# A fused three-layer block with a mixture of experts: ring places of the expert weights by order of release, and a row table made by products

## The reference

```python
pg_top, g_idx = lax.top_k(softmax(hr @ w_rg + b_rg), 1)          # one of 4 groups
pe_top, e_idx = lax.top_k(softmax(sel), 2)                        # two of its 8 experts
order = argsort(expert of each of the 1024 assignments, stable)   # rows by expert
xb = h[tokens of one expert]                                      # gathered rows
y = (silu(xb @ w_gate[e]) * (xb @ w_up[e])) @ w_down[e] * weight  # 32 experts, FF 512
out = zeros.at[token].add(y)
```

## Time and profile before

| | us |
|---|---|
| median of 3 runs | 3084.15 |
| lowest and highest | 3083.63, 3089.73 |
| the profiled execution | 3083.59 |
| its span in the profile | 3081.7 |
| TensorE busy | 2933.5 |
| VectorE busy | 1353.7 |
| ScalarE busy | 1014.0 |
| GpSimd busy | 833.0 |

### The profile page before, as it was taken

One profiled execution on the slowest core, in us unless ns is written; L12 is line 12 of the kernel. 1 busy time (PEld: TensorE's weight loads), 2 busy tenths in 40 slices (PEclk: granted clock), 3 DMA queues, 4 the chain that ended last, 5 costly groups with the idle time before them and its releaser, 6 DMA issues.

```text
span 3081.7 us, 37986 instructions
## 1 busy us (share of the span) xinstructions
PE 2933.5 (95%) x15772; PEld 2119.1 (69%) x15772; DVE 1353.7 (44%) x2292; ACT 1014.0 (33%) x1613; POOL 833.0 (27%) x431
## 2 busy tenths in 40 slices
PE   8999999999996999999999998999999999999996
PEld 6687778886675776877788777787788773333332
DVE  4443230113788754232301224143522338887884
ACT  4454442333772323334423324313332320000000
POOL 3122234442231000222344422202244421211110
PEclk9999999999998899999999999999999999999998
DMA  3341222322120002312223232111133359999995
GB/s 128 97 149 57 67 82 96 96 96 80 51 73 15 2 2 91 122 61 63 96 96 96 96 96 82 55 42 55 56 101 103 129 209 416 406 400 402 412 408 220
DMA packets 207402, 416.43 MB, mean 135 GB/s; under 512 B 16358, under 2 KB 186374, under 8 KB 194304
## 3 DMA queue, kind: packets, MB, share of 16 engines
q1 hardware_dynamic: 190992, 389.05, 34.5%
q0 software_dynamic: 16096, 24.94, 2.3%
q10 hardware_dynamic: 144, 0.01, 0.0%
HBM read 501.70 MB, written 16.79 MB: 168 GB/s over the span
## 4 chain that ended last, share of the span: by engine, by line
PE 80%; DVE 7%; DMA 7%; ACT 3%; issue 2%; POOL 1%; SPq 0%; ACTq 0%; POOLq 0%; DVEq 0%
PE product_banks L650 14%; PE product_banks L651 14%; PE product_banks L652 14%; PE product_banks L2361 7%; PE product_banks L2391 4%; DMA A<-in_w_down 4%; PE product_banks L745 2%; PE product_banks L618 2%; DMA X<-in_w_down 1%; PE product_banks L1693 1%; PE score_banks L1285 1%; PE stat_bank L877 1%; PE product_banks L1695 1%; PE product_banks L1694 1%; PE product_banks L1306 1%
## 5 line engine op out<-in xcount | busy, mean ns | idle before, releaser
L547 POOL TENSOR_TENSOR Wr_parts<-Wr,Wr_parts 128x1024 fp32r<-128x1024 f32 (+3 forms) x223 | 524.7, 2354 | 1054.3 <-ACT Wr_parts L524 1054.2
L651 PE MATMUL product_banks<-A_parts,Wr_parts 128*128 128x512 f32 x1480 | 580.3, 392 | 0.0
L524 ACT ACTIVATE Wr_parts<-Wr 128x1024 fp32r<-128x1024 f32 (+3 forms) x223 | 228.6, 1027 | 620.6 <-PE product_banks L652 569.2
L2443 DVE STREAM_TRANSPOSE Wr<-Wr 32x128 f32<-32x128 f32 (+1 forms) x752 | 388.1, 516 | 16.5 <-DMA Wr<-token_rows,from_row 5.3
L2361 PE MATMUL product_banks<-A,Wr 128*64 128x512 f32 x1328 | 338.3, 599 | 10.0 <-DMA A<-in_w_up 8.8
L651 PEld LDWEIGHTS product_banks<-A_parts,Wr_parts 128*128 128x128 f32 x1480 | 280.9, 190 | 58.0 <-issue 1.0
L650 PE MATMUL product_banks<-H_parts,Wr_parts 128*128 128x512 f32 x744 | 297.1, 399 | 3.5 <-POOL Wr_parts L547 3.5
L650 PE MATMUL product_banks<-A_parts,Wr_parts 128*128 128x512 f32 x736 | 291.9, 397 | 5.7 <-POOL Wr_parts L547 2.8
L652 PE MATMUL product_banks<-H_parts,Wr_parts 128*128 128x512 f32 x744 | 291.5, 392 | 0.0
L652 PE MATMUL product_banks<-A_parts,Wr_parts 128*128 128x512 f32 x736 | 288.6, 392 | 0.0
L547 POOL TENSOR_TENSOR shared_con_parts<-Wr,shared_con_parts 128x1024 fp32r<-128x1024 f32 (+3 forms) x83 | 191.3, 2305 | 341.9 <-ACT shared_con_parts L524 341.9
(11 more groups left out here) (540 smaller groups left out, 4768.6 us busy)
## 6 DMA issues: line engine op xcount, KB each, us to landing
A<-in_w_gate SPq DMA_DIRECT2D x29, 2048.0 KB, 13.7
A<-in_w_up SPq DMA_DIRECT2D x28, 2048.0 KB, 18.1
A<-in_w_down SPq DMA_DIRECT2D x28, 2048.0 KB, 14.5
Wr<-in_m_w_up SPq DMA_DIRECT2D x32, 1024.0 KB, 5.1
Wr<-in_m_w_down SPq DMA_DIRECT2D x32, 1024.0 KB, 4.8
Wr<-in_w_in SPq DMA_DIRECT2D x32, 1024.0 KB, 5.6
Wr<-in_c_w_kv SPq DMA_DIRECT2D x12, 1024.0 KB, 5.1
Wr<-in_b_w_rkv SPq DMA_DIRECT2D x12, 1024.0 KB, 4.8
```

The costliest lines, as they stand in the source:

```text
L524: nc.scalar.activation(weight_parts(s)[0], loaded_part(s), ACT.Copy).then_inc(*mark("weights_high", s))
L547: nc.gpsimd.tensor_tensor(lo, loaded_part(s), hi, ALU.subtract).then_inc(*mark("weights_split", s))
L651: pe.matmul(bank[:, :], hi[:, k, :], x_lo, start=False, stop=False)
L2443: ins = nc.vector.transpose(dst[32 * c:32 * c + 32, :].rearrange("p (k t) -> p k t", k=n)[:, :, rows], src[rows, 32 * n * c:32 * n * (c + ...
```

## The change

Four things are changed.

1. The row table is made on the chip. VectorE makes a matrix of ones and zeros for the place within a column (`AT_PLACE`) and one for the column, times the token's number (`IN_COLUMN`), and TensorE multiplies them (`row_ids_pe`, 8 products of 24 columns). The eight scatters, the table in main memory, its clearing and its reading back are gone.
2. `first_rows_pe` makes the rows of pair 0 in token order, 2 x 4 products of 512 columns; ScalarE copies them to `FIRST_ROWS`, TensorE turns them in 8 transposes, and ScalarE copies them to `XT` as before. `row_ids_pe` stands between the two halves.
3. The ring's places go by pairs to whole stages (`PLACES`, `places_of_stages`): when stage q is done, its pair of places goes to stage q+2 if that is an overflow stage, and otherwise to the next main stage that has none yet.
4. GpSimd waits for `extras_known` after its first two gathers, and VectorE makes `from_row` and `to_row` before the assignments' weights.

```diff
--- before.py
+++ after.py
...
+        IN_COLUMN = tmf[:, 0:8 * NCOL].rearrange("p (j c) -> p j c", j=8)
+        AT_PLACE = flat[:, 4096:5120].rearrange("p (j s) -> p j s", j=8)
+        FIRST_ROWS = shared[:, 1024:2048]
...
             link(dve, nc.vector.tensor_reduce(COLUMN, STEPS, AX_X, ALU.add))
-            link(dve, nc.vector.tensor_scalar(COLUMN, COLUMN, 1.0 - P * NCOL, None, ALU.mult))
-            link(dve, nc.vector.scalar_tensor_tensor(out=COLUMN, in0=DS, scalar=float(NCOL),
-                                                     in1=COLUMN, op0=ALU.mult, op1=ALU.add))
-            nc.vector.tensor_copy(rows_of[:, :], COLUMN).then_inc(*mark("rows_known", 0))
+            link(dve, nc.vector.scalar_tensor_tensor(out=PLACE, in0=COLUMN, scalar=float(-P),
+                                                     in1=DS, op0=ALU.mult, op1=ALU.add))
+            link(dve, nc.vector.tensor_scalar(COLUMN, COLUMN, float(CAP), None, ALU.mult))
+            link(dve, nc.vector.tensor_tensor(
+                IN_COLUMN, cc("first")[:, None, 0:NCOL].broadcast_to([P, 8, NCOL]),
+                COLUMN[:, :, None].broadcast_to([P, 8, NCOL]), ALU.is_equal))
+            link(dve, nc.vector.tensor_tensor(
+                IN_COLUMN, IN_COLUMN, cc("token")[:, :, None].broadcast_to([P, 8, NCOL]), ALU.mult))
+            for j in range(8):
+                ins = nc.vector.tensor_scalar(AT_PLACE[:, j, :], cc("place"), PLACE[:, j:j + 1], None,
+                                              ALU.is_equal)
+            ins.then_inc(*mark("rows_known", 0))
...
+            dve.wait_ge(*at("row_ids_formed", 0))
+            link(dve, nc.vector.tensor_scalar(SROW, S2[:, 1, 288:288 + NCOL], NO_ROW, None, ALU.add))
+            link(dve, nc.vector.tensor_scalar(GROW, SROW, float(T), float(-T), ALU.is_ge, ALU.mult))
+            link(dve, nc.vector.tensor_tensor(GROW, GROW, SROW, ALU.add))
+            nc.vector.tensor_copy(to_row[:, :], SROW)
+            nc.vector.tensor_copy(from_row[:, :], GROW).then_inc(*mark("row_ids_ready", 0))
...
-            dve.wait_ge(*at("row_ids_loaded", 0))
...
             pe.wait_ge(*at("first_places_ready", 0))
+            pe.wait_ge(*at("rows_ready", ("h2", TT - 1, 1)))
+            for n in range(2):
+                for m in range(TT):
+                    mm = pe.matmul(BK[:, 2 + n, :], FIRST[:, m, :], HR[:, m, n * T:(n + 1) * T],
+                                   start=(m == 0), stop=(m == TT - 1))
+                mm.then_inc(*mark("first_rows_formed", n))
+                if n == 0:
+                    row_ids_pe(pe)
             pe.wait_ge(*at("rows_ready", ("xr", TT - 1, 1)))
+            for n in range(2):
+                pe.wait_ge(*at("first_rows_kept", n))
             for k in range(8):
-                for m in range(TT):
-                    mm = pe.matmul((B6, B7)[k // 4][:, (k % 4) * P:(k % 4 + 1) * P],
-                                   HR[:, m, k:D:DT], FIRST[:, m, :], start=(m == 0),
-                                   stop=(m == TT - 1))
-            mm.then_inc(*mark("first_rows_formed", 0))
-
-        def ids_pool(pool):
-
-            pool.wait_ge(*at("rows_known", 0))
-            pool.wait_ge(*at("ids_cleared", 0))
+                mm = pe.transpose((B6, B7)[k // 4][:, (k % 4) * P:(k % 4 + 1) * P],
+                                  FIRST_ROWS[:, k:D:DT], ident)
+            mm.then_inc(*mark("first_rows_turned", 0))
+
+        def row_ids_pe(pe):
+
+            pe.wait_ge(*at("rows_known", 0))
             for j in range(8):
-                pool.indirect_dma_start(
-                    out=id_dram, out_offset=bass.IndirectOffsetOnAxis(
-                        ap=rows_of[:, j:j + 1].bitcast(U32), axis=0),
-                    in_=cc("token", j, 1), in_offset=None).then_inc(
-                        *mark("id_scattered", j, 16))
+                mm = pe.matmul(S2[:, 1, 288:288 + NCOL], AT_PLACE[:, j, :], IN_COLUMN[:, j, :],
+                               start=(j == 0), stop=(j == 7))
+            mm.then_inc(*mark("row_ids_formed", 0))
...
-        LOAD_AT = {key: g for g, key in enumerate(LOADS)}
+
+        PLACES = ((2, 3), (4, 5), (6, 0), (1, 7))
+
+        def places_of_stages():
+
+            taken, before = {}, {}
+            is_extra = [PAIRS[b][0] == "extra" for _, b in STAGES]
+            mains = [q for q in range(len(STAGES)) if not is_extra[q]]
+            for n in range(len(PLACES)):
+                taken[mains.pop(0)] = n
+            for q in range(len(STAGES)):
+                then = q + 2 if q + 2 < len(STAGES) and is_extra[q + 2] else \
+                    mains.pop(0) if mains else None
+                if then is not None:
+                    assert then > q
+                    taken[then], before[then] = taken[q], q
+            return ({STAGES[q]: PLACES[n] for q, n in taken.items()},
+                    {STAGES[q]: STAGES[n] for q, n in before.items()})
+
+        PLACE_OF, USED_BEFORE = places_of_stages()
+
+        def place_of(key):
+            return PLACE_OF[key[0:2]][key[2]]
...
+        PLACE_FREE = {2: ("products_done", ("proj2", 7)), 3: ("products_done", ("proj2", 7)),
+                      4: ("low_part_ready", ("merged", 7)), 5: ("low_part_ready", ("merged", 7)),
+                      6: ("products_done", ("proj2", 7)), 0: ("products_done", ("wout2", 7)),
+                      1: ("products_done", ("wout2", 7)), 7: ("turned", ("xr", TT - 1, 1))}
 
         def slot_free(eng, key):
-            g = LOAD_AT[key]
-            if g >= RINGW:
-                kind, b, _ = LOADS[g - RINGW]
-                eng.wait_ge(*at("unit_used", (kind, b)))
+            if key[0:2] in USED_BEFORE:
+                eng.wait_ge(*at("unit_used", USED_BEFORE[key[0:2]]))
             elif "C" in phases:
-                eng.wait_ge(*at(*SLOT_FREE[g]))
+                eng.wait_ge(*at(*PLACE_FREE[place_of(key)]))
...
-            sp.wait_ge(*at("id_scattered", 7))
-            sp.dma_start(row_ids[:, :], id_dram.rearrange("(p c) a -> p (c a)", p=P)).then_inc(
-                *mark("row_ids_loaded", 0, 16))
...
             def extras_in(*stages):
                 for key in LOADS:
-                    g = LOAD_AT[key]
-                    place = LOADS[g - RINGW][0:2] if g >= RINGW else None
-                    if PAIRS[key[1]][0] == "extra" and place in stages:
+                    if PAIRS[key[1]][0] == "extra" and USED_BEFORE[key[0:2]] in stages:
                         load_extra(pool, key)
 
-            pool.wait_ge(*at("extras_known", 0))
-            extras_in(None)
             pool.wait_ge(*at("row_ids_ready", 0))
             for m in range(TT):
                 pool.wait_ge(*at(f"h2_stored{m}", 0))
             rows_in_pool(pool, 1)
             rows_in_pool(pool, 2)
+            pool.wait_ge(*at("extras_known", 0))
             for b in range(len(PAIRS)):
...
-            act.wait_ge(*at("first_rows_formed", 0))
+            for n in range(2):
+                act.wait_ge(*at("first_rows_formed", n))
+                nc.scalar.activation(FIRST_ROWS[:, n * T:(n + 1) * T], BK[:, 2 + n, :],
+                                     ACT.Copy).then_inc(*mark("first_rows_kept", n))
+            act.wait_ge(*at("first_rows_turned", 0))
...
-            act.dma_start(id_dram.rearrange("(p c) a -> p (c a)", p=P), LB[:, 0, 0:NCOL]).then_inc(
-                *mark("ids_cleared", 0, 16))
...
-                nc.vector.memset(LB[:, :, :], 0.0).then_inc(*mark("zeros_set", 0))
```

More of the change, by code:

```diff
@@ L2246, in program @@
         LOADS = [(kind, b, h) for kind, b in STAGES for h in range(halves(b))]
-        LOAD_AT = {key: g for g, key in enumerate(LOADS)}
+        PLACES = ((2, 3), (4, 5), (6, 0), (1, 7))
[16 more added lines that the diff above has]
+            return PLACE_OF[key[0:2]][key[2]]
         def unit_slot(key):
-            place = (2, 3, 4, 5, 6, 0, 1, 7)[LOAD_AT[key] % RINGW]
+            place = place_of(key)
             return X[:, :, :] if place == 7 else A[:, 8 * place:8 * place + 8, :]
@@ L2281, in load_main @@
             sp.dma_start(unit_rows(key), src).then_inc(
-                *mark(f"unit_loaded{LOAD_AT[key] % RINGW}", key, 16))
+                *mark(f"unit_loaded{place_of(key)}", key, 16))
         def load_extra(pool, key):
@@ L2292, in load_extra @@
                 bounds_check=NE * P - 1, oob_is_err=False).then_inc(
-                *mark(f"extra_loaded{LOAD_AT[key] % RINGW}", key, 16))
+                *mark(f"extra_loaded{place_of(key)}", key, 16))
         def rows_in_pool(pool, b):
@@ L2534, in mlp_act @@
                         rectified(j)
-                    if tag == "m0" and "D" in phases and h == 0 and j == 1:
-                        clear_ids(act)
                     if h and j >= 8 and memory_ahead(tag):
@@ L3752, in _ @@
         def _(act):
-            if "D" in phases and "A" not in phases:
-                clear_ids(act)
             act.wait_ge(*at("constants_set", 0))
```

20 lines of the change are left out of this document (1 added, 19 removed).

## The result

The changed kernel takes 3184.7 us in the median of five runs (3178.3 to 3204.5), against 3084.15 for the kernel before (3082.2 to 3089.7): a ratio of 1.032 [1.030, 1.034], 3.2% slower. The forecast was 3157 in a range from 3085 to 3190.

What follows compares the result with a forecast made beforehand. TensorE and the DMA engines were both taken as near their limit, 61.8 against 61.4 us per nine stages. The sum was 3083.6 - 3.6 - 25.8 + 75.6 + 27.7 = 3157.5, so 3157 us, range 3085 to 3190.

Steps and rivals of the forecast that it cites:

- Step 1: Before the first gate: cheaper first rows and row table start it at about 2528.8 instead of 2532.39, 3.6 us gained.
- Step 2: Expert loop: main loads leave earlier, so 23.7 us of weight waits and 2.1 of clock go, 25.8 us gained.
- Step 3: Expert loop: overflow loads leave only one stage before use, so gate and down stages wait, 103 us lost.
- the eighth pair: Last overflow pair of the expert loop: no main load behind it any more, so it costs nothing.
- The waits: TensorE's waits for overflow loads: down 8.0 us, gate 2.5, up 0; first pair's gate 11.5 and down 12.
- The 14.7: Overflow pair in a loaded queue: its second load is there 14.7 us after the first issue.
- The clock: Stages after long waits run at a lower clock: 2.1 us charged per down wait and twice for the first pair.
- No waits: Rival for the overflow loads: they land within 6.5 us of issue, nothing is lost, 3054 us; chance 0.12.
- Drained queue: Rival: stalls keep the main queue short, each gate and down waits 1.8 us, 3103 us; chance 0.19.
- Worse: Rival: gate and down both find a loaded queue each time, 3180 to 3206 us; chance 0.05.
- The queue rule: DMA engines alternate one for one between GpSimd's and main loads' packets; eight turns take one main load, 4.9 us.

Runs made afterwards that it cites:

- the last experiment: Changed kernel without the 42 loads of unused overflow units, the first overflow pair's three stages taking places four stages ahead: 3065.2 us, ratio 0.994.
- the run with one: Changed kernel, loads of overflow units 1 to 14 covering 16 rows instead of 128, one packet per DMA engine instead of eight: 3112.5 us, ratio 1.009.
- the runs with shorter turns: Changed kernel, each main load issued as two DMAs of 8 KB a row (3155.5 us) or four of 4 KB (3111.0 us) instead of one of 16 KB.

## Why the prediction came out as it did

The sign, the mechanism and the place were right; the loss was 101 us where I had said 73. By its own steps:

- **Step 1, start, 3.6 gained: 4.4.** The products came near their prices: 3.7 us for four of 512 (said 3.4), 1.97 for eight of 24 (2.1). Nothing waited for VectorE ahead of the table's products, where I had allowed 0.4, and the handovers cost next to nothing of the 0.7 put in for them. What the step left out is the first gate stage: I kept its 8.6 us of the kernel before, and it took 6.9, so the start gave 6.1 in all.
- **Step 2, main loads, 25.8 gained.** In the changed kernel all 23.7 us of these waits are gone, as said. But there the stalls themselves gave the transfers time. Without stalls (the last experiment) the loop is 525.8 - 510.2 = 15.6 us shorter. Of these, 1.7 are the first stage's, and 4.9 stand in the kernel before without its empty loads as well (520.9), so some 9 are left for the order. The step was oversized: the first blocks stay bound by transfers.
- **Step 3, overflow loads, 103 lost: 134.** The stages that wait (down, gate, not up), the eighth pair with nothing, and the first gate's wait (12.4, said 11.5) came as written. With the start shifted by 16.8, the first overflow gate came at 2575 (said 2576), in part by luck: TensorE was ready 2.3 us before its time and the load left 2.5 before its own, and the two cancel. Two sizes in the step failed. *The waits:* down 9.5 us in the mean of pairs two to seven (8.9 to 10.4), said 8.0; gate 3.6, said 2.5; the first down 14.2, said 12. Together 105.4 for 86.5. In the last two rows below the first load leaves 0.8 us after its stage's end instead of 0.4, and the second is there 16.4 us after that instead of 14.7 (2806.39 less 2789.96): 0.8 + 16.4 - 6.9 = 10.3, and the wait was 10.36. The 14.7 came from a gate pair. The down pairs two to seven of the kernel before took 14.3 to 16.1 us from the first issue to the second landing, 15.4 in the mean, and those of the changed kernel 14.9 to 16.4 to TensorE's start, 15.6 in the mean. So the new order did not slow them: I had read the wrong pair. The first row below is from the kernel before, 2787 to 2789.5, where the second down load leaves 1.3 us behind the first; the others are from the changed kernel.

```profile
DMA to landing us min/median/max: 10.8/12.6/14.4
```

```profile
2789.96 1.01 POOL L2322 DMA_INDIRECT A<-in_w_down,wrow  x1 [4.74 <-PE product_banks L2388]
...
2806.39 1.08 PE L2418 MATMUL product_banks<-A,Wr 128*64 128x512 f32 x1 [10.36 <-DMA X<-in_w_down,wrow]
```

- *The clock:* I charged 2.1 us to the waits of 7 us and more and nothing to the gate waits. The stages behind waits took 29.0 us more, said 16.8. The gate waits of 3.4 to 4.3 us cost 1.7 to 3.0 us each (gate and up 15.65 to 16.93 instead of 13.91), the down waits 1.4 to 3.0. I had put the limit by two rows, 7.34 with a loss and 2.92 without, and took the value between them for free.
- The sum: 3083.6 - 6.1 - 25.8 + 134.4 = 3186.1, and the measured 3184.7.
- **The rivals.** "No waits" is refuted in the changed kernel, and is what the kernel does once the empty loads are away. "Drained queue" holds for the gate waits alone, which are twice as long as it had them. "Worse" (both find a loaded queue, 3180 to 3206) had the time, but not the cause: the gate loads found a queue that ran out 7 us after they left, DMA share 0.24 behind their wait.

The queue rule stands as the traces had it. In the changed kernel, both DMA queues from 2716 to 2723 (packets, MB, share of 16 engines), as in the earlier trace rows:

```profile
q1 hardware_dynamic: 202, 3.05, 102.1%
q0 software_dynamic: 203, 0.03, 2.6%
```

202 packets against 203: one for one. The Trainium skill says that an engine drains a packet of some 9 to 17 descriptors before it switches ("DMA: Bandwidth & Descriptors", Queues, rings and completion order). No run here shows that: eight small transfers cost eight turns, by the run with one (6.2 us), by the runs with shorter turns, and by the counts of both queues.

Open: what the first down load's 14.2 us of wait is made of, beside carrying weights, and what happens in the 4 us or so between a load's issue and its first packet, which may be most of the 5.1 us that a load with a single packet on each engine takes at least in a loaded queue. The best version that keeps the computation whole is the new start with the old ring, 0.2% faster than before; that with 16 rows and three stages of lead, 0.4%, would need the true number of rows for units in use.

## What to carry to other kernels

```profile
2818.53 8.69 PE L2418 MATMUL product_banks<-A,Wr 128*64 128x512 f32 x32 [2.24 <-DMA A<-in_w_down,wrow]
...
3013.71 7.09 PE L2418 MATMUL product_banks<-A,Wr 128*64 128x512 f32 x32 [2.33 <-DMA A<-in_w_down,wrow]
```
